# Two attention loops: maxima ahead of the preceding step's normalising on VectorE, exponentials ahead of its copy on ScalarE

## The chip, the cores and the metric

The kernel runs on one core of one Trainium2 chip. The metric is the device time of one execution in microseconds (us); lower is better. The time before is 1713.09 us, the median of 3 runs (1712.9 to 1713.82).

## The reference, cut to what matters

Two transformer blocks are computed one after the other on 256 tokens of width 1024, all in fp32. The change touches the two places where attention is computed.

The first block has differential attention (4 heads with two softmaxes each, one subtracted from the other with a factor lambda) and windowed attention with a sink (8 query heads, 2 key heads, own tokens and context tokens). Both see 512 keys:

```python
s = jnp.einsum('bqhcd,bkhcd->bhcqk', q, k)
p = jax.nn.softmax(s, axis=-1)
a = p[:, :, 0] - lam * p[:, :, 1]                      # differential
p = jax.nn.softmax(jnp.concatenate([s_loc, s_ctx, sink_col], axis=-1), axis=-1)   # windowed, with a sink
```

A mixture of 32 experts (top 4) follows; its weights are streamed from HBM. The second block has three attentions over at most 256 keys: block attention (8 heads), sliding window attention with sinks (8 heads) and attention over a memory (4 heads). A gated feed-forward part with a convolution ends it. Each softmax is: maximum over the keys, exponential of the difference with its sum, division by the sum, product with the values.

## The kernel before, in words

Each engine has a program of its own (the blocks `tensor`, `scalar`, `vector`, `gpsimd`, `sync`), works through it in order, and is held by semaphore waits. PE stands for TensorE, ACT for ScalarE, DVE for VectorE.

**First attention loop.** It has N_AT = 16 steps: steps 0 to 7 are differential (N_DA = 8), steps 8 to 15 windowed. A step is one tile of 128 queries and one pair of heads, so two score tiles of 128 x 512. Its life on the engines:

1. `scores` (L681 to L700, PE): two matmuls into the PSUM banks 4 + 2b and 5 + 2b, b = a % 2. From step 2 on they wait for the exponentials of step a-2, which read the same banks.
2. `maxima` (L1701 to L1716, DVE): waits for the scores; for windowed steps adds the mask (L1708); reduces both tiles (L1710), in windowed steps takes the sink in (L1714), and writes the negative maxima (L1712 or L1716), which releases ACT.
3. Exponentials (L1306, ACT), two, with their sums, and in windowed steps two small ones for the sink (L1310).
4. `normalise` (L1718 to L1733, DVE): reciprocal of the sums and scaling. In a differential step both tiles are combined and released together (L1725), in a windowed step each tile is released by its own L1732.
5. `turn_bank` (L702 to L713, PE): four transposes into PSUM bank 2. A windowed step has two such turns, one for each tile.
6. `copy_turn` (L1277 to L1285, ACT): copies bank 2 to SBUF.
7. `values` (L715 to L734, PE): the product with the values.

The order of the work is written out by hand, one loop for each engine, and the steps are staggered. The loop of PE is at L757 to L778. In turn a it does `scores(a)`, then a filler if there is one, `turn_bank(a-1)`, `ada_rows` for turns 8 to 15 (64 small matmuls of the modulation; `ada_rows`, L596 to L606), `values(a-2)`, the second turn of a-1, and `ada_turn` (L612). The filler stands ahead of `turn_bank(a-1)`: it is `project` in turns 0 to 4 (in turn 4 it is only four transposes, L636, whose result ACT copies at L1252) and `memory_job` in turns 5 to 7. Turns 8 to 15 have nothing between `scores(a)` and `turn_bank(a-1)`. In turns 7 and 11 four more transposes (`turn_bank("y", ...)`) end the turn.

The loop of ACT is at L1297 to L1337, that of DVE at L1735 to L1757. ACT also copies the row of the modulation (`ada_copy`, L1210), for which `ada_turn` waits, and in turns 6 and 10 takes a square root (L1316), which loads another table. DVE also does the rotary embedding (`rope`), the lower halves of weights (L1630), and in turns 5, 6, 9 and 10 the norm of the differential output (L1751, L1755, L1756).

The SP queue loads the weights of `ada_rows` and of what follows (L497); each load waits until PE is through with the ring slot's old content.

**Second attention loop.** It has N_C = 24 steps: 0 to 7 block attention, 8 to 15 memory attention (one tile a step), 16 to 23 sliding window with sink. The parts have the same order: `scores_c` (L1037), `maxima_c` (L1933: L1945 adds the bias, L1947 reduces, L1949 and L1950), exponentials (L1505, L1509), `normalise_c` (L1953: L1960, L1962, L1964), `turn_c` (L1056, transposes at L1065), `copy_turn_c` (L1485, L1491), `values_c` (L1068). PE's loop (L1103 to L1113) puts the filler `project_c` between `scores_c(a)` and `turn_c(a-1)` in turns 0 to 12 and 18 to 21, and `branch` in turns 22 to 25. Turns 13 to 17 have no filler. At turn 13 (BIAS_STEP) `maxima_c` first shuffles the second bias table (L1940). DVE also makes the lower halves of the weights in this loop (L1894), ACT the upper halves (L1435).

Of the kernel before, what the change touches and what calls it, by code (L numbers as in the profile page):

```python
# [128 lines left out]
def build(nc, io, out):  # L129
    ctx = ExitStack()  # L130
    with ctx:
# [57 lines left out]
        def col(name):  # L189
            at, width = SMALL_AT[name]  # L190
            return small[:, at:at + width]
# [187 lines left out]
        N_DA, N_AT = 8, 16  # L379

        def step_a(a):

            return (a // 4, a % 4) if a < N_DA else ((a - N_DA) % 2, (a - N_DA) // 2)
# [15 lines left out]
        def turn(kind, a, c=0):  # L399
            return TURNS.index((kind, a, c))  # L400

        ADA_STEP = 5

        KV_STEP = len(JOBS) - EARLY
        ADA_STEP = KV_STEP + 3
# [5 lines left out]
        def kv_at(a):  # L411

            return a - KV_STEP if KV_STEP <= a < ADA_STEP else None

        def ada_at(a):

            return 4 + a - ADA_STEP if ADA_STEP <= a < ADA_STEP + 8 else None
# [5 lines left out]
        C_EARLY, N_C = 6, 24  # L423
# [3 lines left out]
        def c_filler(a):  # L427


            return C_EARLY + a if a < 13 else (C_EARLY + a - 5 if 18 <= a < 22 else None)  # L430
# [737 lines left out]
        def _(act):  # L1168
# [37 lines left out]
            def ada_copy(n, bank):  # L1206
                act.wait_ge(ada_mm, n + 1)
                if n >= 2:
                    act.wait_ge(ada_t, n - 1)
                A(modrow[:, n % 2], ps[:, bank, 0:P], ACT.Copy).then_inc(ada_row, 1)  # L1210
# [66 lines left out]
            def copy_turn(kind, s, c=0):  # L1277
                act.wait_ge(pt_mm, turn(kind, s, c) + 1)
                src = ps[:, 2, :].rearrange("p (a b) -> p a b", a=4)
                if kind == "y":  # L1280
                    A(yT[:, 0:4, P * s:P * s + P], src, ACT.Copy, scale=subln_s[:, 0:1]).then_inc(pt_set, 1)
                else:
                    if s >= 2:
                        act.wait_ge(pv_mm, s - 1)
                    A(pT_a[s % 2][:, c], src, ACT.Copy).then_inc(pt_set, 1)  # L1285
# [9 lines left out]
                    A(v_me[:, i], ps[:, bank, :], ACT.Copy).then_inc(kv_act, 1)  # L1295

            for a in range(N_AT + 2):  # L1297
                if ADA_STEP <= a <= N_AT:
                    copy_turn("p", a - 1)
                if a < N_AT:  # L1300
                    b, j = a % 2, step_a(a)[1]
                    act.wait_ge(max_set, a + 1)
                    if a >= 2:
                        act.wait_ge(pt_mm, turn("p", a - 2, int(a - 2 >= N_DA)) + 1)
                    for c in range(2):
                        A(e_a[:, b, c], ps[:, 4 + 2 * b + c, :], ACT.Exp, bias=negm[:, b, c:c + 1], scale=QK_SCALE,  # L1306
                          accum_out=esum[:, b, c:c + 1]).then_inc(exp_set, 1)
                    if a >= N_DA:
                        for c in range(2):
                            A(esink[:, b, c:c + 1], col("sink")[:, 2 * j + c:2 * j + c + 1], ACT.Exp,  # L1310
                              bias=negm[:, b, c:c + 1]).then_inc(sinkexp_set, 1)
                if ada_at(a) is not None:
                    ada_copy(ada_at(a), 1)
                if a in (6, 10):
                    act.wait_ge(oms_set, a // 6 if a == 6 else 2)
                    A(oss[:], oss[:], ACT.Sqrt).then_inc(oroot_set, 1)  # L1316
                if EARLY + a < len(JOBS):
                    copy_job(EARLY + a)
                if kv_at(a) is not None:
                    copy_memory(kv_at(a))  # L1320
                if 1 <= a < ADA_STEP:
                    copy_turn("p", a - 1)
                if a - 2 in (3, 7):
                    act.wait_ge(pv_mm, a - 1)
                    if a - 2 == 7:
                        act.wait_ge(pt_mm, turn("y", 0) + 1)
                    A(y_da, ps[:, 3, :], ACT.Copy).then_inc(ov_set, 1)
                    act.wait_ge(ov_set, (a - 2) // 4 + 1)
                    A(o_sq, y_da, ACT.Square).then_inc(osq_set, 1)
                if N_DA < a <= N_AT:  # L1330
                    copy_turn("p", a - 1, 1)
                if a - 2 >= N_DA:
                    qt, j = step_a(a - 2)
                    act.wait_ge(pv_mm, a - 1)
                    A(yT[:, 4 + j, P * qt:P * qt + P], ps[:, 3, 0:P], ACT.Copy).then_inc(pv_set, 1)
                if a in (7, 11):
                    copy_turn("y", a // 8)  # L1337
# [147 lines left out]
            def copy_turn_c(s):  # L1485
                kind, j, qt, keys, heads = step_c(s)
                nk = keys // P
                act.wait_ge(c_pt, s + 1)
                if s >= 2:
                    act.wait_ge(c_pv, s - 1)  # L1490
                A(pT_c[s % 2][:, 0:heads, 0:nk, :], ps[:, 2, 0:P * heads * nk].rearrange("p (a b c) -> p a b c", a=heads, b=nk),  # L1491
                  ACT.Copy).then_inc(c_pts, 1)

            for a in range(N_C + 2):
                if c_filler(a) is None and 1 <= a <= N_C:
                    copy_turn_c(a - 1)
                if a < N_C:
                    kind, j, qt, keys, heads = step_c(a)
                    b = a % 2
                    act.wait_ge(c_max, a + 1)  # L1500
                    if a >= 2:
                        act.wait_ge(c_pt, a - 1)
                    for c in range(heads):
                        src = s_c[:, b, c, 0:keys] if kind < 2 else ps[:, 4 + 2 * b, 0:keys]
                        A(e_c[:, b, c, 0:keys], src, ACT.Exp, bias=negm[:, b, c:c + 1],  # L1505
                          scale=MEM_SCALE if kind == 2 else 1.0, accum_out=esum[:, b, c:c + 1]).then_inc(c_exp, 1)
                    if kind == 1:
                        for c in range(heads):
                            A(esink[:, b, c:c + 1], col("swa_sink")[:, 2 * j + c:2 * j + c + 1], ACT.Exp,  # L1509
                              bias=negm[:, b, c:c + 1]).then_inc(c_sink, 1)  # L1510
                if c_filler(a) is not None:
                    split_hi(c_filler(a) + 1)
                    copy_c(c_filler(a))
                    if a >= 1:
                        copy_turn_c(a - 1)
                if a >= 2:
                    kind, j, qt, keys, heads = step_c(a - 2)
                    act.wait_ge(c_pv, a - 1)
                    A(oT[kind][:, j, P * qt:P * qt + P], ps[:, 3, 0:P], ACT.Copy).then_inc(c_pvs, 1)
# [61 lines left out]
        def _(dve):  # L1581
# [151 lines left out]
                                        ALU.mult).then_inc(p_set, 1)  # L1733

            for a in range(N_AT + 1):  # L1735
                if a >= 1:
                    normalise(a - 1)
                if a < N_AT:
                    maxima(a)
                if a == 0:  # L1740
                    dve.wait_ge(lame_set, 1)
                    link(V.tensor_tensor(lamv[:, 0:1], lamv[:, 3:4], lamv[:, 2:3], ALU.subtract))
                    link(V.tensor_scalar(lamv[:, 1:2], lamv[:, 0:1], -LAM_INIT, None, ALU.add))
                if EARLY + a < len(JOBS):
                    rope(EARLY + a)
                if ada_at(a - 1) is not None:
                    ada_columns(ada_at(a - 1), 0)
                heads = lambda x: x.rearrange("p (a b) -> p a b", a=4)
                if a in (5, 9):
                    dve.wait_ge(osq_set, a // 4)  # L1750
                    link(V.tensor_reduce(oss[:], heads(o_sq), AX.X, ALU.add))  # L1751
                    V.tensor_scalar(oss[:], oss[:], 1.0 / P, EPS, ALU.mult, ALU.add).then_inc(oms_set, 1)
                if a in (6, 10):
                    dve.wait_ge(oroot_set, a // 5)
                    link(V.reciprocal(oss[:], oss[:]))  # L1755
                    V.tensor_tensor(heads(y_da), heads(y_da), oss[:].unsqueeze(2).to_broadcast([P, 4, P]),  # L1756
                                    ALU.mult).then_inc(yda_set, 1)  # L1757
# [231 lines left out]
                                x_hi[:, 2 * i:2 * i + 2].bitcast(F32), ALU.subtract).then_inc(mg_lo_set, 1)  # L1989

            for a in range(N_C + 1):
                if a >= 1:
                    normalise_c(a - 1)
                if a < N_C:
                    maxima_c(a)
                if c_filler(a) is not None:
                    split_lo(c_filler(a) + 1)
                if a >= BR_STEP:
                    merge(a - BR_STEP)
# [167 lines left out]
```

## Time and profile before

| | |
|---|---|
| median of 3 runs | 1713.09 us |
| the profiled execution's own time | 1714.07 us |
| its span in the profile | 1712.3 us |
| chain that ended last, by engine | PE 58%, DMA 34%, DVE 4%, ACT 2%, issue 1% |
| PE busy | 1593.6 us (93%) |
| DVE busy | 544.3 us (32%) |
| ACT busy | 442.7 us (26%) |
| first attention loop, in the span | about 108 to 226 us |
| expert stage | about 278 to 1200 us |
| second attention loop, in the span | about 1277 to 1434 us |

Times in the rows are microseconds from the start of the span. "L1710" is line 1710 of the kernel. A row of the timeline has: start, length, engine, line, operation, output <- inputs, shapes, count, and in brackets the idle time of that engine before it and what ended it. Rows on PE overlap a little, since matmuls are pipelined and their ends are modelled. PEclk is the granted TensorE clock: 1.00 is 2.4 GHz, 0.50 is 1.2 GHz. "PEld" is the weight load, which overlaps PE.

### The profile page before, as it was taken

The page shows a single profiled execution, that of the slowest core. Times are in us where ns is not written, and L with a number is a line of the kernel's source. Part 1 is how long each engine was busy: PE and PEld are TensorE (multiplying, and loading weights), DVE is VectorE, ACT ScalarE, POOL GpSimd, SP SyncE. Part 2 cuts the span into 40 slices and gives each one's busy share as a digit, 9 for nine tenths or more (in the row PEclk, how much of TensorE's full clock was granted, in tenths as well). Part 3 has the DMA queues.
Part 4 walks back from the last instruction along what each step waited for, and adds up shares of the span by engine and source line. Part 5 has one row for each costly group of instructions (what it writes and reads, how often), then busy time and mean ns, then how long its engine had stood idle before and what let it go on. Part 6 is the DMA issues. An engine that isn't in the chain of part 4 may idle for free.

```text
span 1712.3 us, 23738 instructions
## 1 busy us (share of the span) xinstructions
PE 1593.6 (93%) x10016; PEld 982.3 (57%) x10016; DVE 544.3 (32%) x1090; ACT 442.7 (26%) x854; POOL 7.3 (0%) x16
## 2 busy tenths in 40 slices
PE   5999999999999999999999999998799989899997
PEld 3786676443333343334333433333399978789997
DVE  3754513110101011010101010101355564468863
ACT  3434523010101010011101100000445552455642
POOL 0000000000000000000000000000000100000000
PEclk9999998999999999999999999999899989999999
DMA  9325853999999999999999999999634524425420
GB/s 394 150 91 210 330 173 111 422 437 433 429 429 436 433 429 432 435 432 429 432 435 432 429 433 435 431 429 433 294 123 149 185 99 148 148 99 197 170 102 25
DMA packets 27432, 524.79 MB, mean 306 GB/s; under 512 B 2931, under 2 KB 7027, under 8 KB 7492
## 3 DMA queue, kind: packets, MB, share of 16 engines
q1 hardware_dynamic: 24368, 519.06, 72.9%
q10 hardware_dynamic: 2484, 3.19, 0.7%
q0 software_dynamic: 512, 1.57, 0.4%
q8 instruction: 51, 0.84, 0.2%
q14 instruction: 17, 0.14, 0.0%
HBM read 522.72 MB, written 1.08 MB: 306 GB/s over the span
## 4 chain that ended last, share of the span: by engine, by line
PE 58%; DMA 34%; DVE 4%; ACT 2%; issue 1%; SPq 0%; ACTq 0%; DVEq 0%
PE ps L584 57%; DMA ring<-in_w_down 33%; DMA ring<-in_first 1%; DMA arena<-in_ctxT 1%; DVE mx L1710 1%; PE ps L1065 0%; ACT arena L1306 0%; PE ps L712 0%; DVE arena L1612 0%; DVE nrm L1609 0%; ACT w_high L1435 0%; DVE ring_r L1630 0%; DVE hx_lo L1637 0%; DVE arena L1643 0%; DVE arena L1940 0%
## 5 line engine op out<-in xcount | busy, mean ns | idle before, releaser
L584 PE MATMUL ps<-ring,arena 128*64 128x512 f32 (+1 forms) x3872 | 722.6, 534 | 45.6 <-DMA ring<-in_w_down 31.1
L584 PEld LDWEIGHTS ps<-ring,arena 128*64 128x64 f32 (+1 forms) x3872 | 240.9, 133 | 479.0 <-issue 403.9
L584 PE MATMUL ps<-arena_r,w_high 128*128 128x256 f32 x1840 | 340.4, 287 | 10.2 <-DVE arena_r L1920 9.4
L584 PEld LDWEIGHTS ps<-arena_r,w_high 128*128 128x128 f32 x1840 | 290.6, 194 | 15.1 <-issue 12.8
L584 PE MATMUL ps<-arena 64*128 64x256 f32 (+7 forms) x1780 | 264.9, 382 | 6.3 <-DVE arena L1823 1.6
L584 PE MATMUL ps<-arena_r,ring_r 128*128 128x256 f32 x920 | 262.1, 285 | 0.0
L1847 DVE TENSOR_SCALAR arena<-ps 128x512 f32<-128x512 f32 x32 | 22.1, 692 | 716.2 <-PE ps L584 716.2
L584 PEld LDWEIGHTS ps<-arena 64*128 64x128 f32 (+3 forms) x1780 | 169.1, 178 | 111.5 <-issue 98.1
L584 PEld LDWEIGHTS ps<-arena_r,ring_r 128*128 128x128 f32 x920 | 178.6, 194 | 0.0
L1894 DVE TENSOR_TENSOR ring_r<-ring,w_high 128x1024 fp32r<-128x1024 f32 x120 | 142.0, 1221 | 86.0 <-ACT w_high L1435 86.0
L1435 ACT ACTIVATE w_high<-ring 128x1024 fp32r<-128x1024 f32 x120 | 120.6, 1050 | 26.4 <-PE ps L584 26.4
L1386 ACT ACTIVATE arena<-ps 128x256 f32<-128x256 f32 x32 | 12.3, 383 | 337.1 <-PE ps L911 337.1
L584 PE MATMUL ps<-arena,ring 128*128 128x256 f32 x384 | 84.9, 381 | 1.7 <-ACT arena L1252 0.7
L1381 ACT ACTIVATE arena<-arena 128x512 f32<-128x512 f32 x32 | 20.1, 630 | 238.4 <-DVE arena L1847 238.4
L584 PEld LDWEIGHTS ps<-arena,ring 128*128 128x128 f32 x384 | 72.4, 190 | 13.3 <-issue 3.0
L584 PE MATMUL ps<-arena,ones 128*128 128x256 f32 (+1 forms) x112 | 43.9, 525 | 23.7 <-ACT arena L1199 13.0
L1396 ACT ACTIVATE arena<-ps 128x512 f32<-128x512 f32 x32 | 19.1, 597 | 168.3 <-PE ps L584 168.3
L2042 DVE SCALAR_TENSOR_TENSOR arena<-ps,small,arena 128x255 f32<-128x255 f32 (+1 forms) x88 | 38.4, 478 | 29.5 <-ACT arena L1559 28.7
L584 PE MATMUL ps<-hx_hi,w_high 128*128 128x256 f32 (+1 forms) x112 | 38.9, 347 | 7.3 <-DVE hx_lo L1637 5.0
L584 PEld LDWEIGHTS ps<-arena,ones 128*128 128x128 f32 x112 | 21.3, 217 | 42.1 <-issue 19.9
L1375 ACT ACTIVATE arena<-ps 128x512 f32<-128x512 f32 x32 | 19.1, 597 | 101.1 <-PE ps L584 101.1
L1818 DVE TENSOR_SCALAR arena<-small,rank 128x64 f32<-128x64 f32 x68 | 12.6, 251 | 80.3 <-PE ps L584 80.3
(205 smaller groups left out, 1061.9 us busy)
## 6 DMA issues: line engine op xcount, KB each, us to landing
ring<-in_w_gate_up SPq DMA_DIRECT2D x64, 4096.0 KB, 20.8
ring<-in_w_down SPq DMA_DIRECT2D x32, 4096.0 KB, 19.7
ring<-in_second SPq DMA_DIRECT2D x32, 2048.0 KB, 8.1
ring<-in_first SPq DMA_DIRECT2D x19, 2048.0 KB, 9.5
ring<-in_first SPq DMA_DIRECT2D x3, 1024.0 KB, 4.9
ring<-in_second SPq DMA_DIRECT2D x2, 1024.0 KB, 5.2
small<-in_small ACTq DMA_DIRECT2D x1, 1024.5 KB, 8.1
arena<-in_xT SPq DMA_DIRECT2D x1, 1024.0 KB, 7.9
```

Source lines behind the costliest of these rows:

```text
L584: return nc.tensor.matmul(out_, lhsT, rhs, start=start, stop=stop, **kw)
L1375: A(xg[:, 4 * half:4 * half + 4, :], ps[:, 2, :].rearrange("p (a b) -> p a b", a=4), ACT.Copy).then_inc(S.x_ready, 1)
L1381: A(sig_e, g_e, ACT.Sigmoid, scale=SWIGLU_ALPHA).then_inc(S.sig_ready, 1)
L1386: A(sgt, ps[:, 3, 0:T], ACT.Copy).then_inc(S.sgt_ready, 1)
L1396: A(y_e, ps[:, 3, :], ACT.Copy).then_inc(S.y_ready, 1)
L1435: A(part_hi(n), part_of(n, ring), ACT.Copy).then_inc(w_hi_set, 1)
L1710: link(V.tensor_reduce(mx[:, b], banks, AX.X, ALU.max))
L1818: last = V.tensor_scalar(s_hot[:, t, jj], col("iota_slot")[:, 0:SLOTS], rank[:, t, bass.ds(e0 + jj, 1)], None, ALU.is_equal)
L1847: V.tensor_scalar(two_banks(g_e), hidden[:, :, :, 0], SWIGLU_LIMIT, None, ALU.min).then_inc(S.g_ready, 1)
L1894: V.tensor_tensor(part_of(n, ring_r), part_of(n, ring), part_hi(n).bitcast(F32), ALU.subtract).then_inc(w_lo_set, 1)
L2042: last = V.scalar_tensor_tensor(u[:, c, late:T], src[:, 0:T - late], col("conv_w")[:, 44 * tap + ch:44 * tap + ch + 1], u[:, c, late:T], A ...
```

## The change

Four edits, two in each loop.

- DVE, both loops: `maxima(a)` is issued ahead of `normalise(a-1)`. Before it was the other way round.
- ACT, first loop, turns 8 to 16 (ADA_STEP = 8): the exponentials of step a are issued ahead of `copy_turn("p", a-1)`.
- ACT, second loop: `copy_turn_c(a-1)` always follows the exponentials of step a. Before, this held only in turns with a `project_c`; in the others (13 to 17 and 22 to 24) the copy came first.

PE's order, SP's and POOL's are the same, and no instruction is added or taken away.

```diff
@@ scalar, first loop
             for a in range(N_AT + 2):
-                if ADA_STEP <= a <= N_AT:
-                    copy_turn("p", a - 1)
                 if a < N_AT:
                     b, j = a % 2, step_a(a)[1]
                     act.wait_ge(max_set, a + 1)
...
                             A(esink[:, b, c:c + 1], col("sink")[:, 2 * j + c:2 * j + c + 1], ACT.Exp,
                               bias=negm[:, b, c:c + 1]).then_inc(sinkexp_set, 1)
+                if ADA_STEP <= a <= N_AT:
+                    copy_turn("p", a - 1)
                 if ada_at(a) is not None:
                     ada_copy(ada_at(a), 1)
@@ scalar, second loop
             for a in range(N_C + 2):
-                if c_filler(a) is None and 1 <= a <= N_C:
-                    copy_turn_c(a - 1)
                 if a < N_C:
...
                 if c_filler(a) is not None:
                     split_hi(c_filler(a) + 1)
                     copy_c(c_filler(a))
-                    if a >= 1:
-                        copy_turn_c(a - 1)
+                if 1 <= a <= N_C:
+                    copy_turn_c(a - 1)
@@ vector, first loop
             for a in range(N_AT + 1):
+                if a < N_AT:
+                    maxima(a)
                 if a >= 1:
                     normalise(a - 1)
-                if a < N_AT:
-                    maxima(a)
@@ vector, second loop
             for a in range(N_C + 1):
+                if a < N_C:
+                    maxima_c(a)
                 if a >= 1:
                     normalise_c(a - 1)
-                if a < N_C:
-                    maxima_c(a)
```

## Rows read from the trace of the kernel before

**Rows 1.** Timeline of PE and DVE, turn 13 of the first loop.
```profile
204.63 1.13 PE L584 MATMUL ps<-arena 64*128 64x512 f32 x4
205.69 0.66 PE L712 MATMUL ps<-small,arena 128*128 128x128 f32 x4
205.80 0.43 DVE L1708 TENSOR_TENSOR ps<-ps,small 128x256 f32<-128x256 f32 x1 [0.27 <-PE ps L584]
206.27 1.95 PE L584 MATMUL ps<-ring,arena 128*32 128x128 f32 x64
207.72 0.17 DVE L1716 TENSOR_SCALAR negm<-mx 128x2 f32<-128x2 f32 x1
...
209.18 0.66 PE L712 MATMUL ps<-small,arena 128*128 128x128 f32 x4
...
209.96 0.33 PE L612 MATMUL ps<-small,arena 128*128 128x128 f32 x1
```

**Rows 2.** Timeline of ACT and PE, end of turn 13 and start of turn 14.
```profile
209.27 0.47 ACT L1310 ACTIVATE esink<-small,negm 128x1 f32<-128x1 f32 x2
...
210.22 1.13 PE L584 MATMUL ps<-arena 64*128 64x512 f32 x4
```

**Rows 3.** Timeline of DVE and PE, turn 10: normalising, then the turn that waits for it.
```profile
184.47 0.16 DVE L1729 TENSOR_TENSOR tot<-esum,esink 128x2 f32<-128x2 f32 x1
...
185.50 1.06 PE L712 MATMUL ps<-small,arena 128*128 128x128 f32 x4 [1.57 <-DVE arena L1732]
...
186.49 3.12 PE L584 MATMUL ps<-ring,arena 128*32 128x128 f32 x64
```

**Rows 4.** A window of 1 us in turn 10 (engines' busy time, PEclk, DMA share, GB/s).
```profile
186.00:187.00 1.00, 1.00 (x15) 0.64 (x17) 0.97 (x2) 0.40 (x1) 0.00 (x0) 0.50 1.00 426
```

**Rows 5.** Timeline of DVE and PE, turn 1.
```profile
120.52 0.16 DVE L1722 RECIPROCAL rsum<-esum 128x2 f32<-128x2 f32 x1
...
122.27 0.63 PE L712 MATMUL ps<-small,arena 128*128 128x128 f32 x4
```

**Rows 6.** Timeline of PE and DVE, turns 4 and 5.
```profile
140.16 1.23 DVE L1710 TENSOR_REDUCE mx<-ps 128x2 f32<-128x1024 f32 x1 [1.26 <-PE ps L584]
...
140.53 0.60 PE L712 MATMUL ps<-small,arena 128*128 128x128 f32 x4
...
141.42 0.17 DVE L1712 TENSOR_SCALAR negm<-mx 128x2 f32<-128x2 f32 x1
...
143.81 7.14 PE L584 MATMUL ps<-arena,ring 128*128 128x256 f32 x32 [0.72 <-ACT arena L1252]
```

**Rows 7.** Timeline of PE: scores of step 8, and first turn of step 15.
```profile
171.62 1.13 PE L584 MATMUL ps<-arena 64*128 64x512 f32 x4
...
222.06 0.63 PE L712 MATMUL ps<-small,arena 128*128 128x128 f32 x4 [0.59 <-DVE arena L1732]
```

**Rows 8.** Chain of waits, second loop: one turn with a filler (start, us, what).
```profile
1296.76 6.95 PE ps L584 x56
```

**Rows 9.** Timeline of DVE, PE and ACT, turns 13 to 18 of the second loop.
```profile
1369.74 3.75 DVE L1940 STREAM_SHUFFLE arena<-arena 128x3072 f32<-128x3072 f32 x1
...
1375.24 0.42 DVE L1947 TENSOR_REDUCE mx<-ps 128x1 f32<-128x256 f32 x1
...
1375.72 1.04 PE L584 MATMUL ps<-arena 128*128 128x128 f32 x6
...
1379.78 0.42 DVE L1945 SCALAR_TENSOR_TENSOR arena<-ps,arena 128x256 f32<-128x256 f32 x1 [0.17 <-PE ps L584]
1380.21 2.22 PE L584 MATMUL ps<-arena 128*128 128x128 f32 x8
...
1381.09 0.40 ACT L1505 ACTIVATE arena<-arena,negm 128x128 f32<-128x128 f32 x1 [0.25 <-DVE negm L1950]
...
1383.47 0.66 PE L1065 MATMUL ps<-small,arena 128*128 128x128 f32 x2 [1.04 <-DVE arena L1964]
...
1385.64 0.79 PE L584 MATMUL ps<-arena_r,w_high 128*128 128x256 f32 x2
```

## The prediction

> **What bounds the kernel now.** I read four views, in this order. The page's chain by engine says that TensorE ends 58% of the span and DMA 34%; the DMA share lies in the expert stage, which the change doesn't touch. The chain of waits, restricted to the two attention loops, shows where TensorE isn't the end. The timeline of all engines then gives the order inside one turn, and windows give the granted clock.
>
> In turns 8 to 15 of the first loop a turn takes 5.59 us (scores 13 start at 204.63, scores 14 at 210.22) and TensorE is at work for nearly all of it: its only wait is about 0.19 us ahead of `ada_turn` at 209.96, since the transposes ahead of it, begun at 209.18, take 0.58 (as from 205.69 to 206.27) [rows 1, 2]. The reader is to see in [rows 1] that the transposes of step 12 (L712, 205.69) start as the scores of step 13 end, 0.11 us ahead of the mask at 205.80: `normalise(12)` was done while TensorE computed scores 13. The chain of waits does run through maxima and exponentials there, but only because they lead to `ada_copy`; it says nothing of slack to be won. In turns with a filler TensorE works without a break: 7.14 us of it in turn 5 [rows 6], 6.95 us in a turn of the second loop [rows 8].
>
> **Part 1: VectorE in turns 8 to 15.** TensorE's order stays: scores(a), then the turn of step a-1. That turn needs `normalise(a-1)`, which now stands behind `maxima(a)`, which needs scores(a). So nothing of it lies beside TensorE any more, and there is no filler in between. The price, from rows: from the mask's start at 205.80 to the last small instruction at 207.72, plus 0.08 till the next may follow, 2.00 us [rows 1]. From the start of `normalise` to the transposes that wait for its first half, 184.47 to 185.50, 1.03 us [rows 3]. The transposes would start at 205.80 + 2.00 + 1.03 = 208.83, not 205.69: 3.14 us later. The 0.19 us wait goes. A turn is then 5.59 + 3.14 - 0.19, so 8.55 us. Queued behind the wait on TensorE are `ada_rows`, `values(a-2)`, the second transposes, `ada_turn` and scores(a+1): all shift.
>
> Turn 8 normalises a differential step, which takes 1.75 us to the transposes (120.52 to 122.27) [rows 5] in place of 1.03, but has no second transposes: 8.62. Turn 10 is held a little by the norm of the differential output on VectorE, which reaches 0.4 us past the scores' end: 8.95. Turn 11 has four more transposes behind a copy: about 1.2 more, 9.73; both are estimates from the durations in [rows 1]. From scores 8 to the first turn of step 15 I get 8.62 + 8.55 + 8.95 + 9.73 + 4 x 8.55 = 70.05 us; before it is 222.06 - 171.62 = 50.44 [rows 7]. **+19.6 us.** The square roots and their table loads, which lengthened turns 10 and 11 before, now lie beside the new wait; that is counted.
>
> **Part 2: turns 1 and 4.** In turn 1 `normalise(0)` starts at 120.52 and ends just as the filler does (transposes at 122.27) [rows 5]: no slack. Maxima first costs 1.34 us (140.16 to 141.42, plus 0.08, for the same work [rows 6]). **+1.3 us.** In turn 4 the filler is four transposes, 0.5 us. Maxima 4 wait for scores till 140.16; `normalise(3)` follows at 141.50, the transposes at 141.50 + 1.75 = 143.25 and not 140.53, 2.72 later. Of that 0.80 was waited for anyway at the memory product of 143.81 [rows 6]. **+1.9 us.** Turns 2, 3 and 5 to 7 cost nothing: a filler of 5.6 to 7.1 us lies ahead of the transposes, against 1.34 + 1.75 us on VectorE and the rotary work between; without that cover each would cost 3 us.
>
> **Part 3: TensorE's clock.** In turn 10 TensorE waited 1.57 us for `normalise` [rows 3], and right behind it the granted clock is 0.50, the 1.2 GHz level [rows 4]. `ada_rows` took 3.12 us there against 1.95, and the four transposes 1.06 against 0.66 [rows 1, 3]: 1.57 us lost in one stretch. The new wait is twice as long and comes every turn, so I take one such stretch a turn: 8 x 1.57, **+12.6 us**. From below it is 0 (the clock stays), from above two stretches a turn, 25.1. I take the middle one because the nearest row is of just this place with a shorter wait. The Trainium skill (TensorE: Matmul & The Clock Gate, HAM oscillation) describes just such a loop, with the loss paid in each iteration; but its rule asks for a gap longer than the one forecast here, so by it the clock would be kept and the sum would be 12.6 us less. The trace differs from the rule: 1.57 us of waiting were enough.
>
> **Part 4: the second loop.** Turns 1 to 12 and 18 to 25: 4 to 7 us of filler ahead of the transposes [rows 8] against at most 3 us on VectorE; the weights' lower halves, now behind `normalise_c`, wait for ScalarE anyway. Nothing. Turns 13 to 17 have no filler. In turn 13 the shuffle of 3.75 us [rows 9] now comes ahead of `normalise_c(12)`: shuffle till about 1373.05, maxima 0.6, normalising and release 0.7, transposes 12 at 1374.3. From there, by the same order: values and scores 1.0 (1375.72 row), maxima 0.62, normalise 0.69, transposes 0.25, 2.55 a turn, so transposes 14 at 1379.4. Values 13 and scores 16 take about 2.2 at the lower clock (1380.21 row), maxima 16 1.3 (1379.78 to 1381.09), normalising 0.7, transposes 0.66 (1383.47 row), again 2.2, then maxima 17 1.85, normalising 1.03, transposes 0.66, 1.8: the filler of turn 18 starts at 1391.4, not 1385.64 [rows 9]. **+5.8 us**; with the clock kept 2.7, with one more slow stretch 7.5.
>
> **Part 5: ScalarE and the queues.** The exponentials now precede the copy. In turns 9 to 15 they and the sink's end some 4 us after the mask's start (205.80 to 209.74) [rows 1, 2]; the copy then takes 0.6 and is wanted 3.5 us after the new start of the transposes: hidden, the spare is 2 us. Without it the second transposes would be late. `ada_copy` waits for `ada_rows`, which is later still. No DMA is moved; SP's loads wait for `ada_rows` and go later with it, which leaves DMA more room. POOL's order is untouched.
>
> **Sum.** 19.6 + 1.3 + 1.9 + 12.6 + 5.8 = +41.2 us, against the profiled execution (1714.07, span 1712.3) 1755.3; against the median of 1713.09, which lies 1.0 below, 1754.3. The expert stage starts that much later, since its first free slots hang on TensorE's work behind the loop.
>
> **Rivals.**
> A, the clock stays up: 19.6 + 1.3 + 1.9 + 2.7 = +25.5, 1738.6 us. For it: the new wait breaks each turn just once, and work on both sides is dense. Against it: [rows 3, 4]. The rule of the skill named above would give this time. Chance 0.18.
> B, the clock stays down for most of the loop, since no turn is dense enough to bring it back: 22.8 + 25.1 + 7.5 = +55.4, 1768.5 us. For it: in turns 14 to 17 of the second loop the matmuls stay at the slow pace (8 in 2.22 us against 6 in 1.04) over several waits [rows 9]. Against it: there TensorE has little work a turn. Chance 0.17.
> C, faster: maxima(a) start earlier wherever VectorE, not the scores, was late, the exponentials with them, and `normalise(a-1)` is still done before TensorE asks. That takes at least 2.00 + 1.03 us of TensorE work between scores(a) and the transposes; in turns 8 to 15 there is none, and this decides. If it held, turns 8 to 15 would run at TensorE's own 5.4 us, 50.4 - 43.8 = 6.6 us less, and turns 13 to 17 of the second loop about 6 less: 1700.5 us. Chance 0.03.
> D, the order doesn't matter, because the wait that appears on TensorE only replaces that at `ada_turn`: 1713 us. It would need the two to be of one size; they are 3.14 and 0.19. Chance 0.03.
>
> **How the numbers follow.** The forecast, 1754.3, has 0.59. The range takes in A and B with little beyond: 1737 to 1769. No difference under 0.2% (3.4 us) can be told from none. Faster by more: 0.03 (C); within: 0.03 (D); slower: 0.94.
>
> **What would show it.** In the new profile: L712 in turns 8 to 15 waits for L1732 (L1725 in turn 8) each time, about 3 us; scores start every 9 to 10.5 us; the clock of the stretch is about 0.8; L712 of turn 4 waits for L1725; L1065 waits in turns 13 to 17 only; turns with fillers are as before. A mask (L1708) that doesn't start with the scores' end, or transposes that don't wait, would prove the account wrong; a clock of 1.00 would leave A, one near 0.5 B.

## The result, and the profile after

The changed kernel takes 1756.17 us (median of 4 runs, 1755.88 to 1758.98) against 1713.45 us for the kernel before in the runs beside it: ratio 1.0252, 95% interval 1.0234 to 1.0269. It is 42.7 us slower; the forecast was 1754.3 us, 41.2 us slower. The profiled execution took 1755.92 us, its span is 1754.0 us.

The chain that ended last, by engine, and the granted clock of the first loop from step 8 on, as a window of the whole stretch (columns: stretch, length, busy time of PE, PEld, DVE, ACT, POOL with counts, granted clock, DMA share, GB/s). Before, the stretch from scores 8 to the output product (171.62 to 226.91) had a granted clock of 0.97:

```profile
PE 59%; DMA 33%; DVE 5%; ACT 2%; issue 1%; SPq 0%; ACTq 0%; DVEq 0%
```

```profile
172.00:257.00 85.00, 58.34 (x751) 41.93 (x749) 28.73 (x80) 32.13 (x85) 0.00 (x0) 0.84 0.52 186
```

The lines of VectorE have numbers two lower than before (L1706 is the mask, L1708 the maxima, L1714 the last small instruction, L1723, L1727 and L1730 normalise, L1962 normalises in the second loop). The timeline of turns 13 and 14 answers to [rows 1]:

```profile
228.39 1.13 PE L584 MATMUL ps<-arena 64*128 64x512 f32 x4
232.60 0.63 PE L712 MATMUL ps<-small,arena 128*128 128x128 f32 x4 [3.08 <-DVE arena L1730]
233.16 1.95 PE L584 MATMUL ps<-ring,arena 128*32 128x128 f32 x64
236.07 0.66 PE L712 MATMUL ps<-small,arena 128*128 128x128 f32 x4
236.56 0.27 PE L612 MATMUL ps<-small,arena 128*128 128x128 f32 x1
236.76 1.13 PE L584 MATMUL ps<-arena 64*128 64x512 f32 x4
240.97 1.05 PE L712 MATMUL ps<-small,arena 128*128 128x128 f32 x4 [3.08 <-DVE arena L1730]
241.95 3.14 PE L584 MATMUL ps<-ring,arena 128*32 128x128 f32 x64
246.05 0.66 PE L712 MATMUL ps<-small,arena 128*128 128x128 f32 x4
246.54 0.27 PE L612 MATMUL ps<-small,arena 128*128 128x128 f32 x1
246.74 1.13 PE L584 MATMUL ps<-arena 64*128 64x512 f32 x4
```

The transposes, which before started as the scores ended, now wait 3.08 us for VectorE, and the next scores start 8.37 us (turn 13) or 9.98 us (turn 14) after the preceding ones, not 5.59. The two turns have the same wait; they differ in `ada_rows`, 1.95 against 3.14 us. Windows of 1 us show why: behind the wait turn 13 has the full clock, turn 14 (and turn 12, the first window) the half one.

```profile
222.00:223.00 1.00, 1.00 (x15) 0.64 (x17) 0.00 (x0) 0.78 (x3) 0.00 (x0) 0.50 0.00 0
...
233.00:234.00 1.00, 1.00 (x35) 0.84 (x36) 0.00 (x0) 0.99 (x5) 0.00 (x0) 1.00 0.15 49
...
242.00:243.00 1.00, 1.00 (x21) 0.94 (x24) 0.00 (x0) 0.60 (x1) 0.00 (x0) 0.50 0.04 16
```

VectorE in turn 12 answers to [rows 3]: `tot` starts 2.00 us after the mask, and the transposes follow 1.03 us behind it.

```profile
218.42 0.43 DVE L1706 TENSOR_TENSOR ps<-ps,small 128x256 f32<-128x256 f32 x1 [7.86 <-PE ps L584]
...
220.42 0.16 DVE L1727 TENSOR_TENSOR tot<-esum,esink 128x2 f32<-128x2 f32 x1
...
221.45 1.09 PE L712 MATMUL ps<-small,arena 128*128 128x128 f32 x4 [3.08 <-DVE arena L1730]
```

Turns 1 and 4 answer to [rows 5, 6], in a timeline of PE:

```profile
123.63 0.66 PE L712 MATMUL ps<-small,arena 128*128 128x128 f32 x4 [1.13 <-DVE arena L1723]
...
144.70 0.63 PE L712 MATMUL ps<-small,arena 128*128 128x128 f32 x4 [2.60 <-DVE arena L1723]
145.16 3.66 PE L584 MATMUL ps<-arena 128*128 128x128 f32 x12
148.75 1.60 PE L584 MATMUL ps<-arena,ring 128*128 128x256 f32 x6
```

Turns 12 to 17 of the second loop answer to [rows 9] (turn 12 is the last with a filler):

```profile
1405.38 0.38 PE L1065 MATMUL ps<-small,arena 128*128 128x128 f32 x2
...
1409.27 0.41 PE L1065 MATMUL ps<-small,arena 128*128 128x128 f32 x2 [2.63 <-DVE arena L1962]
...
1411.82 0.66 PE L1065 MATMUL ps<-small,arena 128*128 128x128 f32 x2 [1.26 <-DVE arena L1962]
...
1415.44 0.66 PE L1065 MATMUL ps<-small,arena 128*128 128x128 f32 x2 [1.25 <-DVE arena L1962]
...
1419.61 0.66 PE L1065 MATMUL ps<-small,arena 128*128 128x128 f32 x2 [1.93 <-DVE arena L1962]
...
1425.06 0.66 PE L1065 MATMUL ps<-small,arena 128*128 128x128 f32 x2 [2.79 <-DVE arena L1962]
```

Each of the five turns without a filler has its wait. The first is longer because the shuffle lies ahead of the maxima (L1938, 3.71 us from 1404.31), the last two because the sliding window's maxima take more instructions. From the second wait on the transposes take 0.66 us, the pace of the half clock.

Where the time went, by the start of the same work in both traces:

| work | before | after | shift |
|---|---|---|---|
| transposes of turn 1 | 122.27 | 123.63 | +1.4 |
| memory product of turn 5 | 143.81 | 148.75 | +4.9 |
| scores of step 8 | 171.62 | 176.63 | +5.0 |
| output product behind the first loop | 226.91 | 262.25 | +35.3 |
| first transposes of the second loop | 1289.57 | 1324.61 | +35.0 |
| the piece of the chain of waits that holds turn 18's filler | 1384.13 | 1425.72 | +41.6 |
| end of the span | 1712.3 | 1754.0 | +41.7 |

The expert stage between the loops only moved, and so did all that follows turn 18.

### The profile page after: what moved, and what is told of

Its sections match the earlier page's. It is cut to its first block, busy times and chain, and to the rows that moved or that the text cites. A ratio compares the mean times of both kernels' runs of the same rounds, so it can differ in the third digit from the quotient of the medians.

```text
span 1754.0 us, 23738 instructions
## 1 busy us (share of the span) xinstructions
PE 1605.4 (92%) x10016; PEld 991.1 (57%) x10016; DVE 543.9 (31%) x1090; ACT 444.9 (25%) x854; POOL 7.2 (0%) x16
## 3 DMA queue, kind: packets, MB, share of 16 engines
q0 software_dynamic: 512, 1.57, 0.4%
## 4 chain that ended last, share of the span: by engine, by line
PE 59%; DMA 33%; DVE 5%; ACT 2%; issue 1%; SPq 0%; ACTq 0%; DVEq 0%
PE ps L584 57%; DMA ring<-in_w_down 32%; PE ps L712 1%; DVE mx L1708 1%; DMA ring<-in_first 1%; DMA arena<-in_ctxT 1%; PE ps L1065 0%; DVE ring_r L1628 0%; DVE arena L1610 0%; DVE nrm L1607 0%; ACT w_high L1435 0%; DVE hx_lo L1635 0%; DVE arena L1641 0%; DVE arena L1938 0%; DVE arena L1730 0%
## 5 line engine op out<-in xcount | busy, mean ns | idle before, releaser
L584 PEld LDWEIGHTS ps<-ring,arena 128*64 128x64 f32 (+1 forms) x3872 | 246.6, 137 | 480.5 <-issue 404.5
L1396 ACT ACTIVATE arena<-ps 128x512 f32<-128x512 f32 x32 | 19.1, 597 | 168.2 <-PE ps L584 168.2
L712 PE MATMUL ps<-small,arena 128*128 128x128 f32 x104 | 18.8, 311 | 30.8 <-DVE arena L1730 22.0
L1375 ACT ACTIVATE arena<-ps 128x512 f32<-128x512 f32 x32 | 19.1, 597 | 101.0 <-PE ps L584 101.0
```

Source lines behind the costliest of these rows:

```text
L584: return nc.tensor.matmul(out_, lhsT, rhs, start=start, stop=stop, **kw)
L712: last = nc.tensor.transpose(ps[:, 2, P * kt:P * kt + P], src[:, P * kt:P * kt + P], ident)
L1375: A(xg[:, 4 * half:4 * half + 4, :], ps[:, 2, :].rearrange("p (a b) -> p a b", a=4), ACT.Copy).then_inc(S.x_ready, 1)
L1396: A(y_e, ps[:, 3, :], ACT.Copy).then_inc(S.y_ready, 1)
```

## The experiments

In each diff "-" is the kernel named first. Times of before are those of the runs on the same chip. Of single profiles I compare the starts of work, since the expert stage alone differs by some us between executions (see the last section).

### Which engine's edit: VectorE's alone, ScalarE's alone

Against before; the first takes only the two edits of the vector block, the second only those of the scalar block.

```diff
 # vector, both loops
+                if a < N_AT:
+                    maxima(a)
                 if a >= 1:
                     normalise(a - 1)
-                if a < N_AT:
-                    maxima(a)
```

> VectorE's order of the change in both loops, ScalarE's as before. Theory (the loss is all VectorE's: normalise(a-1) waits behind maxima(a) for scores(a), and TensorE waits for it): the same time as with the whole change, 1754 to 1758 us; the exponentials then stand behind a copy that comes late, but nobody asks for them before the next turn. Rival (ScalarE's order carries a part of the loss, since it puts the copy, for which the second transposes wait, behind 1.8 us of exponentials): below 1750 us.

Measured: 1756.56 us (1756.42 to 1757.81), before 1714.82; ratio 1.0243 (1.0226 to 1.0260). The output product behind the first loop starts at 262.20, as with the whole change (262.25). All of the loss is VectorE's edit; the rival falls. That the two starts are equal is chance: in this profile turn 4 keeps the full clock, so that scores 8 start at 174.93 and not 176.63, and then every one of the eight turns has a stretch at the half clock, where the whole change has six. Like turns take the same time: one with the 3.08 us wait and one slow stretch takes 9.98 us in both.

```diff
 # scalar, first loop
-                if ADA_STEP <= a <= N_AT:
-                    copy_turn("p", a - 1)
                 if a < N_AT:
...
+                if ADA_STEP <= a <= N_AT:
+                    copy_turn("p", a - 1)
                 if ada_at(a) is not None:
                     ada_copy(ada_at(a), 1)
```

> ScalarE's order of the change in both loops, VectorE's as before. Theory: alone it costs, since the first transposes are early here and only their copy is now late: exponentials and sink end 5.11 us after the scores' start, the copy 0.6 later, so the second transposes start at about 5.9 and not 4.55, and a turn takes 6.7 us in place of 5.59: some 6 turns x 1.1, 1719 to 1722 us. Inside the whole change this cost is hidden behind VectorE's. Rival (ScalarE's edit is harmless, or a gain through earlier exponentials): 1711 to 1715 us.

Measured: 1723.35 us (1718.39 to 1725.87), before 1714.82; ratio 1.0035 (1.0019 to 1.0052). The timeline of PE in turns 13 and 14 shows the mechanism:

```profile
209.60 0.66 PE L712 MATMUL ps<-small,arena 128*128 128x128 f32 x4
210.19 1.95 PE L584 MATMUL ps<-ring,arena 128*32 128x128 f32 x64
214.20 0.66 PE L712 MATMUL ps<-small,arena 128*128 128x128 f32 x4 [1.03 <-ACT arena L1285]
```

The first transposes are on time, the second wait 1.03 us for the copy, and a turn takes 6.36 us (scores at 208.54, 214.90, 221.25). The output product starts at 233.22, 6.3 us late. So ScalarE's edit isn't harmless in itself: it costs 6.3 us alone and nothing beside VectorE's. The two don't add up, since the same stretch is late already. The median is 1.4 us above the range given. In the profile, the slowest of the eight runs, the rest of the loss is 5.6 us in the expert stage and nothing in the second loop; how much of the 8.5 us of the median lies there the other runs don't show.

### Which loop

The change in the first loop only, and in the second only (the same edits, one loop left as before).

> The change in the first loop only. Theory: the losses of the loops are apart and add up; the first has 35 us (the product behind the loop starts at 262.25 in place of 226.91): 1747 to 1751 us. Rival (the delay of the first loop is partly won back in the expert stage, whose loads hang on DMA, and the second loop has more than its 6.6 us): below 1745 us.

Measured: 1748.72 us (1747.4 to 1751.35), ratio 1.0198 (1.0180 to 1.0217); the output product at 261.30.

> The change in the second loop only. Theory: 6.6 us, all of it in the five turns without a filler: 1719 to 1721.5 us, with the first TensorE work of turn 0 where it was. Rival: as in the run above, with the rest: over 1723 us.

Measured: 1720.38 us (1720.03 to 1722.8), ratio 1.0035 (1.0021 to 1.0049). The first loop's output product is at 226.90, as before; from the first transposes of the second loop (here and below the start of their weight load) to the piece with turn 18's filler it is 1390.01 - 1288.7 = 101.3 us, before 1384.13 - 1289.5 = 94.6. The losses are 33.9 and 5.6 us by the medians, 39.5 together against 42.7 for the whole change. In the traces they are 34.4 and 6.7, together 41.1 against 35.3 + 6.6 = 41.9; most of what is missing lies ahead of scores 8, which start at 175.69 here and not at 176.63, since turn 4 kept the full clock. So the losses of the loops add up within the scatter of the runs.

### Which turns

VectorE's order only in the turns whose filler lies ahead of the transposes (2, 3, 5, 6 and 7 of the first loop, 0 to 12 and 18 to 23 of the second, edited likewise), and only in turns 1 and 4 of the first loop:

```diff
 # vector, first loop; COVERED is a in (2, 3, 5, 6, 7), in the second kernel a in (1, 4)
+                if a < N_AT and COVERED:
+                    maxima(a)
                 if a >= 1:
                     normalise(a - 1)
-                if a < N_AT:
+                if a < N_AT and not COVERED:
                     maxima(a)
```

> Maxima first on VectorE, but only in the turns with a filler of over 4 us ahead of the transposes (turns 2, 3, 5, 6, 7 of the first loop; 0 to 12 and 18 to 23 of the second); ScalarE as before. Theory: the same as before, within 1.5 us, since TensorE doesn't wait in those turns either way. Rival (earlier exponentials free ScalarE and VectorE for the weights' halves, so the filler turns gain): over 2 us faster.

Measured: 1714.55 us (1714.11 to 1720.19), before 1714.27; ratio 1.0004 (0.9992 to 1.0017). Scores 8 start at 171.51, the output product at 226.84. In these turns (23 without turn 0 of the second loop, which has nothing to normalise) the order makes no difference, for the better or the worse.

> Maxima first on VectorE in turns 1 and 4 of the first loop alone, all else as before. Theory by the terms of the prediction: 1.3 + 1.9 us; in the changed kernel the same two turns cost 4.9, with a stretch at the lower clock. So 3.2 to 5 us, and the memory product of turn 5 starts at 147 to 149 us. Rival (the two waits are absorbed in the fillers behind them): no difference.

Measured: 1718.39 us (1716.7 to 1721.41), 4.1 us more; ratio 1.0021 (1.0009 to 1.0032). The memory product starts at 147.21, 3.4 us late, the output product at 230.17, 3.3 late. These are the 1.3 and 1.9 us of the prediction; in this execution no slow stretch came with them.

### Filling the wait with work that is there

On top of the whole change, TensorE's order in turns 8 to 15:

```diff
 # tensor, first loop, turns 8 to 15
-                if 1 <= a <= N_AT:
-                    turn_bank("p", a - 1)
                 if ada_at(a) is not None:
...
                     ada_rows(ada_at(a), 1)
-                if a >= 2:
+                    values(a - 2)
+                if 1 <= a <= N_AT:
+                    turn_bank("p", a - 1)
+                if a >= 2 and ada_at(a) is None:
                     values(a - 2)
```

> The whole change, and on TensorE, in turns 8 to 15, ada_rows(a) and values(a-2) issued ahead of the transposes of step a-1, so that they fill the new wait. Theory: a turn of the stretch falls from 10.1 to some 6.5 us (now the copy behind the exponentials holds the second transposes), the clock stays up, and the whole is 1724 to 1731 us: most of the loss was uncovered waiting. Rival (the longer turns have another cause, such as VectorE and ScalarE being in each other's way at PSUM): over 1745 us.

Measured: 1732.76 us (1728.08 to 1735.97), ratio 1.0104 (1.0067 to 1.0140). The waits of a turn in its timeline:

```profile
213.52 0.63 PE L712 MATMUL ps<-small,arena 128*128 128x128 f32 x4 [0.17 <-DVE arena L1731]
...
214.97 0.66 PE L712 MATMUL ps<-small,arena 128*128 128x128 f32 x4 [0.82 <-ACT arena L1286]
```

Of 3.08 us 0.17 is left, the copy behind the exponentials takes 0.82, a turn takes 6.35 us (209.31 to 215.66) and the output product starts at 233.89. That is 28.4 us earlier than with the whole change, of which 1.5 are turn 4, which kept the full clock here (scores 8 at 175.12, not 176.63). So from scores 8 on 26.9 of the 30.3 us lost were waiting that nothing covered, with the clock that it cost. The median is 1.8 us above the range that I gave; the profiled execution, 1729.76 us, lies in it. It doesn't reach the time before the change.

### Filling the wait with work that is of no use: what the clock costs

On top of the whole change; the six matmuls write a bank that the transposes then overwrite, so the output is the same.

```diff
 # tensor, first loop
+                if ada_at(a) is not None:
+                    pe.wait_ge(pt_set, turn("p", a - 1))
+                    for _ in range(6):
+                        mm(ps[:, 2, 0:T], qa[:, 0, 0:P], ka[:, 0, 0:T], True, True)
                 if 1 <= a <= N_AT:
                     turn_bank("p", a - 1)
```

> The whole change, and in turns 8 to 15 six more matmuls (128 x 256, their result is overwritten) between the scores and the transposes: they take 2.7 us at the full clock, so they fit the wait of 3.08 us and lengthen nothing in themselves. Theory (the waits cost the clock as well): the granted clock is 1.00 over the stretch and the time falls by 10 to 12 us, to 1744 to 1747 us, with a turn of 8.3 us. Rival (the slow matmuls are not due to the waits): no gain, 1755 to 1758 us.

Measured: 1747.49 us (1745.43 to 1749.98), ratio 1.0184 (1.0152 to 1.0215). That is 33.2 us above its kernel before, where the whole change was 42.7 above its own: 9.5 us less, where 10 to 12 were expected, and 0.5 above the range of the time. The stretch as a window, and a turn:

```profile
172.00:257.00 85.00, 78.82 (x915) 58.76 (x914) 28.97 (x82) 35.30 (x92) 1.81 (x1) 1.00 0.58 198
```

```profile
228.72 3.92 PE L584 MATMUL ps<-arena 64*128 64x512 f32 x16
...
232.93 0.63 PE L712 MATMUL ps<-small,arena 128*128 128x128 f32 x4 [0.29 <-DVE arena L1734]
233.49 1.95 PE L584 MATMUL ps<-ring,arena 128*32 128x128 f32 x64
```

The granted clock is 1.00, every `ada_rows` takes 1.95 us, a turn 8.37 (220.35 to 228.72), as long as turn 13 of the changed kernel, so the six matmuls lengthen nothing. Scores 8 start at 176.63 in both traces, the output product at 250.99 and not 262.25: **the lower clock cost 11.3 us** of the first loop in this profile. The same stretch, 74.36 us here and 85.62 with the whole change, takes 87.27 with VectorE's edit alone and 85.31 in the run with the shuffle in turn 10 (below), so by this measure the clock cost 10.9 to 12.9 us from one execution to another. The median shows less of it: in this profile the part from there to the second loop took 1317.5 - 250.99 = 1066.5 us, in that of the whole change 1324.6 - 262.25 = 1062.4. What is left against before, (250.99 - 176.63) - (226.91 - 171.62) = 19.1 us, is the waiting. The kernel before had a slow stretch of its own in turn 10 in its profile; it hardly enters, since turns 10 and 11 take 16.24 us there and 16.02 in the profile of the change in the second loop only, where the clock stayed up.

### The shuffle of the second loop

`BIAS_STEP = 10` in place of 13, on the kernel before and on the changed one.

> The kernel before, with the shuffle of the second bias table in turn 10 of the second loop (which has a filler) and not in turn 13. Theory (in turn 13 the shuffle of 3.75 us holds TensorE, since nothing covers it; in turn 10 VectorE has some 3.4 us to spare): 2 to 5 us faster, 1708.5 to 1712 us, and from the shuffle's old turn to the filler of turn 18 TensorE needs 10 to 12.5 us in place of 14.2. Rival (the shuffle then delays the weights' lower halves, or waits for its loads): no gain or a loss.

Measured: 1711.93 us (1710.75 to 1713.53), before 1714.24; ratio 0.9986 (0.9976 to 0.9995). From the first transposes of the loop to the piece with turn 18's filler it takes 1382.87 - 1290.6 = 92.3 us in place of 94.6.

> The whole change with the shuffle in turn 10. It tells how much of the second loop's 6.6 us is the shuffle's, behind which the transposes of step 12 now wait. Theory: 2 to 4 us less than the whole change, so in turns 13 to 17 the order still costs some 5 us against the kernel before with the same shuffle: the loss is that of the waits, not of the shuffle. Rival (the shuffle is the cause): the second loop as fast as in the run above.

Measured: 1752.61 us (1750.35 to 1756.7), ratio 1.0232 (1.0214 to 1.0249). The same stretch takes 1420.23 - 1323.6 = 96.6 us, with the shuffle in turn 13 1425.72 - 1324.5 = 101.2. So with the shuffle out of the way the order still costs 96.6 - 92.3 = 4.3 us; the shuffle had a share of 2.3 in the 6.6. Most of what moving it gives the changed kernel is clock: of the 4.6 us (101.2 to 96.6) 1.4 are the shorter first wait (1.26 in place of 2.63), 3.2 come behind it, where the matmuls are now at the full pace. The waits in this trace:

```profile
1406.99 0.41 PE L1065 MATMUL ps<-small,arena 128*128 128x128 f32 x2 [1.26 <-DVE arena L1962]
1409.54 0.41 PE L1065 MATMUL ps<-small,arena 128*128 128x128 f32 x2 [1.25 <-DVE arena L1962]
1412.09 0.41 PE L1065 MATMUL ps<-small,arena 128*128 128x128 f32 x2 [1.26 <-DVE arena L1962]
1415.29 0.41 PE L1065 MATMUL ps<-small,arena 128*128 128x128 f32 x2 [1.92 <-DVE arena L1962]
1419.57 0.66 PE L1065 MATMUL ps<-small,arena 128*128 128x128 f32 x2 [2.79 <-DVE arena L1962]
```

A memory attention turn takes 2.55 us, the figure of the prediction, and behind four of the five waits the transposes keep the full pace (0.41).

### A version that beats both

On the kernel before, VectorE's sums and scaling of the differential norm one turn later each, alone and with the shuffle in turn 10:

```diff
 # vector, first loop
-                if a in (5, 9):
-                    dve.wait_ge(osq_set, a // 4)
+                if a in (6, 10):
+                    dve.wait_ge(osq_set, a // 5)
...
-                if a in (6, 10):
+                if a in (7, 11):
                     dve.wait_ge(oroot_set, a // 5)
```

> The kernel before with the later sums and scaling of the differential norm alone. Theory: 2.5 to 4.5 us faster, all of it between the scores of steps 10 and 12. Rival: within 1 us of before.

Measured: 1714.57 us (1710.61 to 1717.63), ratio 0.9998 (0.9987 to 1.0010). In the trace the output product starts at 223.75, 3.2 us early, and scores 10, 11 and 12 at 182.84, 188.43 and 195.88 (before 182.80, 191.27 and 199.04), as expected; the span is 1709.8. By the medians there is no gain, 2.5 us short of the range and as the rival had it: the runs spread over 7 us, and the profiled one (1711.57) is among the faster. So the gain is shown in the trace alone.

> The kernel before, with the shuffle in turn 10, and on VectorE in the first loop the sums of the differential norm (L1751) one turn later, behind maxima of turns 6 and 10, and its scaling (L1756) behind maxima of turns 7 and 11. Theory: turns 10 and 11, which took 8.47 and 7.77 us because VectorE stood in them for ScalarE's square and root with normalise queued behind, fall to some 6.5 and 7 us, the stretch at the lower clock goes, 2.5 to 4.5 us; with the shuffle 5 to 9 us faster than before, 1704 to 1709 us. Rival (the wait moves to the last transposes of turn 11, which need the scaling): only the shuffle's gain.

Measured: **1708.45 us** (1707.15 to 1709.27), before 1714.24; ratio 0.9966 (0.9951 to 0.9980). The output product is at 223.69 (3.2 us early) and the stretch of the second loop takes 1378.74 - 1286.5 = 92.2 us (2.4 less); together 5.6, and the span is 5.7 shorter. It is 5.8 us by the medians, small but clear of the noise. VectorE is late in turns 10 and 11 because ScalarE's results are awaited there with `normalise` queued behind; that wait is moved, not the order of maxima and normalise.

## Why the prediction was right

Step by step, forecast and measured:

- Turns 8 to 15, waiting: 19.6 us forecast, 19.1 measured (the wait filled with matmuls). The parts hold too: 2.00 + 1.03 us on VectorE are 2.00 + 1.03 in the new trace. Turn 8 takes 8.62 us with the wait filled (176.63 to 185.25), as forecast, and turns 10 and 11 take 8.85 and 9.60, near the forecast. The other turns at the full clock take 8.28 (187.49 to 195.77) to 8.37 us, not 8.55: from the second transposes to the next scores it was 1.04 us before (209.18 to 210.22) and is 0.69 now (236.07 to 236.76), so 0.35 falls away and not 0.19. The last piece, to the first transposes of step 15, takes 9.02 and makes up for a part.
- The clock in these turns: 12.6 forecast, 11.3 measured. The mechanism is right, the rate of one slow stretch a turn partly luck. In the profile of VectorE's edit alone all eight turns have one, of 1.6 us each (turns 13 and 14 take 9.98 and 9.99 us: 226.71, 236.69, 246.68), just as forecast. In the profile of the change turns 9 and 13 have none (`ada_rows` 1.95) and turns 8 and 12 a longer one (3.64). And the row that the rate was read from was one execution: the same 1.57 us wait in turn 10 kept the full clock in two other profiles in which these turns are as before. So "1.57 us of waiting were enough" holds for that execution and is no rule (rows below the list).
- Turn 1: 1.3 forecast, 1.4 measured. Turn 4: 1.9 forecast, 3.6 measured in the profile of the change. The term was too small: behind the 2.60 us wait the clock fell, and 12 matmuls took 3.66 us in place of 2.12. I had counted that stretch in turns 8 to 15 and in the second loop, but not here, where it may come or not: with turns 1 and 4 alone, and the same 2.60 us wait, the two cost 3.4.
- Second loop: 5.8 forecast (its terms as written add up to 6.2), 6.6 measured, with the lower clock earlier than I took it (0.66 from the second wait on): from the transposes of turn 14 to those of turn 15 it is 3.62 us (1411.82 to 1415.44), not 2.55.
- Nothing in the turns with a filler: measured 0.3 us of median and no shift in the trace.
- ScalarE: hidden, and of a cost in itself if VectorE's delay were not there. Both hold: nothing beside VectorE's delay, 6.3 us alone. The signs held too, but scores start every 8.28 to 11.22 us, a wider range than the 9 to 10.5 given.

The 1.57 us wait of turn 10 with the full clock behind it, in the profile of the change in the second loop only (the first loop is as before):

```profile
185.71 0.63 PE L712 MATMUL ps<-small,arena 128*128 128x128 f32 x4 [1.57 <-DVE arena L1730]
186.27 1.95 PE L584 MATMUL ps<-ring,arena 128*32 128x128 f32 x64
```

The errors, -0.5, -1.3, +1.7 (turns 1 and 4) and +0.8, sum to 0.7 us. That the total is so close is in part luck, since errors of 1 to 2 us cancel and single executions differ by as much in the clock alone.

The rivals. A, the clock stays up: 25.5 us forecast for it; it fell at each kind of place, and keeping it up by other work moved the time by 9.5 us. The rule of the Trainium skill (TensorE: Matmul & The Clock Gate, HAM oscillation) that asks for longer gaps doesn't hold in this trace: waits of 2.60 and 3.08 us brought the half clock. What the Trainium skill says there of a loop that pays anew in each iteration fits: six of the eight turns paid in this trace, all eight in that of VectorE's edit alone. B, the clock down for most of the loop: the granted clock over the stretch is 0.84. C, faster: the order gave no gain in the 23 turns where it could do no harm. D, a wait that only replaces another: 3.08 us came and 0.35 went.

## What to carry to other kernels

When two pieces of work on an engine change places, look at what the second engine has queued behind the piece that now comes later, and at what lies between there: here the same exchange cost nothing with 4 us or more of filler and over 3 us a turn without it. A wait on TensorE can be paid for twice, by its length and by the clock behind it (19 and 11 us here, the second part varying from one execution to the next); a test that fills the wait with useless matmuls tells the two apart. A chain through maxima and exponentials doesn't show that they should come earlier: in the regular turns before, TensorE lost no more than 0.35 us to waiting.

## What the runs showed of the hardware

- Waits of one length don't always bring the lower clock. In the changed kernel 3.08 to 3.86 us did in turns 8, 10 to 12, 14 and 15, 3.08 us did not in turns 9 and 13; 2.60 us (2.61) in turn 4 did in the profiles of the change and of the filled wait, and did not in the five others with the same wait there. 1.57 us in turn 10 did in the kernel before, and did not in the profiles of the change in the second loop only and of turns 1 and 4 alone. In the changed kernel with the shuffle in turn 10, waits of 1.26, 1.25, 1.26 and 1.92 us one behind the other kept the full clock, and behind the 2.79 that followed it was lower. Waits of 0.29 us did nothing. What decides between two equal waits was not tried.
- The expert stage isn't of constant length. In the profile of ScalarE's edit alone it took 1301.4 - 233.22 = 1068.2 us from the output product to the second loop, before 1289.5 - 226.91 = 1062.6. What sets it was not tried; it makes medians of kernels that differ by 3 us hard to tell apart (the norm later alone: 1710.6 to 1717.6).
